# Two of four down groups moved to the end of each layer's last Strassen chunk

## The chip, the cores and the metric

The kernel runs on one core of one Trainium2 chip. The metric is the device time of one execution in microseconds (us). The time before is 2076.21 us, the median of 3 runs (2076.1 to 2077.36).

## What is computed

The program is a two-layer encoder over 256 tokens of width 2048, in float32. Layer 0 mixes tokens with a convolution module, layer 1 with latent attention; behind each mixer stands a feed-forward block of inner width 5632. Cut to what matters:

```python
def swiglu(h, w_gate, w_up, w_down):
    return (jax.nn.silu(h @ w_gate) * (h @ w_up)) @ w_down

for i in range(DEPTH):                      # DEPTH = 2
    h = h + mixer_i(rmsnorm(h, attn_norm_g[i]))
    h = h + swiglu(rmsnorm(h, ffn_norm_g[i]), ffn_w_gate[i], ffn_w_up[i], ffn_w_down[i])
return rmsnorm(h, final_norm_g)
```

## The kernel before

Every float32 product is made of three products of rounded halves: high by high, high by low, low by high. A weight group is 128 partitions x 2048 elements (1 MB). SP loads it into a tile (four slots of `raw`, and `row_bc` as a fifth), ScalarE (ACT) makes the high half in `w_hi` (L687), VectorE (DVE) makes the low half in `w_lo` (L874), and TensorE (PE) multiplies (L1367). `w_hi` and `w_lo` have four slots each, used in turn, so the ACT split of a group waits until PE has used the group four places before it.

The feed-forward block runs over 11 chunks of 512 inner columns. Chunk 0 is plain. In each of chunks 1 to 10 the first two quarters of the gate and up products are made by Strassen's scheme with seven products (Q1 to Q7, 12 matmuls each), the other quarters plainly (G2, G3 for gate, U2, U3 for up, 24 matmuls each, 12 for each of the two token tiles), and in between stand the four down groups D0 to D3 (24 matmuls each) that multiply the hidden activations of the chunk before. The order on PE is written out by hand in `chunk` and, as positions, in the list at L89: Q1, Q3, (transposes of the hidden activations of the chunk before), Q5, D0, D1, Q6, D2, Q7, D3, Q2, G2, Q4, G3, U2, U3. ACT and DVE follow orders of their own, also written out by hand. An engine's queue runs strictly in order.

These dependencies touch the change:

- Q5, Q7, Q6 and Q4 use sums of a gate and an up weight group. POOL issues a DMA that adds the second weights onto the first ones where they lie in `raw` (L530). The sum for Q4 is added where Q6's sum lies, so it is issued once DVE has made the low half of Q6.
- After Q6, DVE mixes Strassen results in the PSUM banks (`mix_q1_q6`, L1172 to L1177); Q7 waits for the second of these.
- After Q7, ACT copies bank 1 (`q167`, L740) and DVE subtracts it from bank 3 (`mix_q7`, L1181). PE waits for that (`mixed`, 4n+4) ahead of G2, which goes on writing into banks 0 and 1.
- The results of a down group are added to the residual by DVE (`add`, L1147), two additions a group; each counts in `out_added`. The four groups use PSUM banks 4 to 7 in turn: D0 4 and 5, D1 6 and 7, D2 4 and 5, D3 6 and 7.
- `hidden(c)` on PE transposes the hidden activations into banks 4 and 5. It waits for the whole of `up_mul(c)` (L1139) and, for each bank, for the addition that empties it:

```python
pe.wait_ge(ff_h_done, 4 * (FC * l + c) + 4)
for b in range(2):
    pe.wait_ge(out_added, added + TT * CC * (c - 1) + 5 + b)
```

  With 8 additions a chunk this is the fifth and the sixth one made in the chunk that the down groups of c-1 stand in: those of D2. ACT then copies the transposes into `a_hi` (L716), DVE makes `a_lo` (L1121), and only then the next down group starts.
- Behind chunk 10 PE has `hidden(10)` and then the four last down groups, whose weights are at the positions F_LAST to F_LAST + 3, here FL0 to FL3.

Of the kernel before, what the change touches and what calls it, by code (L numbers as in the profile page):

```python
# [87 lines left out]

Q1, Q3, Q5, D0, D1, Q6, D2, Q7, D3, Q2, G2, Q4, G3, U2, U3 = range(15)  # L89
DOWN = (D0, D1, D2, D3)  # L90
F_CHUNK = 15
F_FIRST = 2 * KG
F_LAST = F_FIRST + F_CHUNK * (FC - 1)
F_ALL = F_LAST + CC
F_RAW = {Q1: 0, Q5: 0, Q6: 0, Q4: 0, Q3: 1, Q7: 1, D0: 4, D1: 2, D2: 3, D3: 4, Q2: 2, G2: 3, G3: 4, U2: 2, U3: 3}


def f_pos(c, p):
    return F_FIRST + F_CHUNK * (c - 1) + p


def f_part(q):
    return (q - F_FIRST) % F_CHUNK


def f_raw(q):

    if q < F_FIRST:
        return q % RING
    return F_RAW[f_part(q)] if q < F_LAST else q - F_LAST  # L110


def f_w(q):
# [45 lines left out]
def encoder(nc, x, positions, attn_norm_g, ffn_norm_g, final_norm_g, conv_w_pw1, conv_b_pw1, conv_w_dw,  # L159
# [3 lines left out]
    with ctx:  # L163
# [192 lines left out]
        def wait_f_lo(eng, l, q):  # L356
            eng.wait_ge(f_lo_done, F_ALL * l + q + 1)

        def wait_f_used(eng, l, q):
            eng.wait_ge(f_used, F_ALL * l + q + 1)  # L360

        def chunk_no(l, c):

            return (FC - 1) * l + c - 1
# [31 lines left out]
        def _(sp):  # L396
# [46 lines left out]
            def ffn_loads(l):  # L443
                wg, wu, wd = ffn_w_gate[l], ffn_w_up[l], ffn_w_down[l]

                def f_load(q, src):
                    before = f_before(q, f_raw)
                    if before is not None:
                        wait_f_lo(sp, l, before)
                    elif q < RING:  # L450
                        wait_lo(sp, G_END[l] - RING + q)
                    elif l == 0:
                        sp.wait_ge(out_added, TT)
                    sp.dma_start(f_raw_tile(l, q).rearrange("p (k n) -> p k n", k=GK), src).then_inc(f_in[f_raw(q)], 16)

                def part(c, p):
                    f_load(f_pos(c, p), w_of(l, p, c))

                for n, w in ((0, wg), (1, wu)):
                    for j in range(KG):  # L460
                        f_load(KG * n + j, tile_rows(w, slice(GK * j, GK * j + GK), slice(0, CH)))
                part(1, Q1)
                part(1, Q3)
                for p in (D0, D1, D2):
                    part(1, p)
                for c in range(1, FC):
                    for p in (D3, Q2, G2):
                        part(c, p)
                    if c < FC - 1:
                        part(c + 1, Q3)  # L470
                    for p in (G3, U2, U3):
                        part(c, p)
                    if c < FC - 1:
                        part(c + 1, Q1)
                        for p in (D0, D1, D2):
                            part(c + 1, p)
                for n in range(CC):
                    f_load(F_LAST + n, w_of(l, DOWN[n], FC))
            ffn_loads(0)

            for j in range(KG):
# [83 lines left out]
        def _(act):  # L565
# [134 lines left out]
            def ffn(l):  # L700

                def gate_sig(c):

                    for t in range(TT):
                        if c > 0 and t == 0:
                            act.wait_ge(tile0_done, 2 * chunk_no(l, c) + 1)
                        else:
                            wait_f_used(act, l, KG - 1 if c == 0 else f_pos(c, G3))
                        act.activation(ff_sig[:, t, :], ps[:, t, :], ACT.Sigmoid,
                                       scale=rstd[:, t:t + 1]).then_inc(ff_sig_done, 1)  # L710

                def hidden(c):

                    for b in range(2):
                        act.wait_ge(ff_tr, 2 * (FC * l + c) + b + 1)
                        act.activation(a_hi[:, 0, 2 * b:2 * b + 2, :].rearrange("p k s -> p (k s)"), ps[:, 4 + b, :],  # L716
                                       ACT.Copy).then_inc(ahi_done, 1)

                def parts_hi(c, *parts):
                    for p in parts:  # L720
                        f_hi(l, f_pos(c, p))

                for q in range(3, F_FIRST):
                    f_hi(l, q)
                act.wait_ge(rstd_ready, RSTD[(2, 5)[l]])
                act.wait_ge(s_sum_done, l + 1)
                act.activation(s_hi[:, :, :, :].rearrange("p n k s -> p (n k s)"), ytmp[:, 1, :],
                               ACT.Copy).then_inc(s_hi_done, 1)
                gate_sig(0)
                parts_hi(1, Q1, Q3, Q5)  # L730
                for c in range(1, FC):
                    parts_hi(c, D0, D1)
                    wait_f_used(act, l, f_pos(c, Q1))
                    act.activation(q1, ps[:, 0, :], ACT.Copy).then_inc(q1_done, 1)
                    hidden(c - 1)
                    wait_f_used(act, l, f_pos(c, Q5))
                    act.activation(q5, ps[:, 3, :], ACT.Copy).then_inc(q5_done, 1)
                    parts_hi(c, Q6, D2, Q7, D3, Q2, G2)
                    wait_f_used(act, l, f_pos(c, Q7))
                    act.activation(q167, ps[:, 1, :], ACT.Copy).then_inc(q167_done, 1)  # L740
                    parts_hi(c, Q4, G3, U2, U3)
                    parts_hi(c + 1, 0)
                    gate_sig(c)
                    if l == 1 and c == FC - 1:
                        wait_f_lo(act, l, f_pos(c, G3))
                        act.dma_start(row_bc[:, :], final_norm_g.rearrange("(a d) -> a d", a=1).to_broadcast([P, D])
                                      ).then_inc(final_g_in, 16)
                    parts_hi(c + 1, 1, 2)
                hidden(FC - 1)
                f_hi(l, F_ALL - 1)  # L750
                if l == 0:

                    end = G_DQ
                    hi(end)
                    chunk_hi(3, 0, R_ATTN + KT)
                    hi(end + 1)
                    chunk_hi(3, 1, R_ATTN + KT)
                    hi(end + 2)
# [99 lines left out]
        def _(dve):  # L858
# [257 lines left out]
            def ffn(l):  # L1116
# [79 lines left out]
                for c in range(1, FC):  # L1196
                    parts_lo(c, D0, D1)
                    hidden(c - 1)
                    parts_lo(c, Q6, D2)
                    add(0, f_pos(c, D0))  # L1200
                    parts_lo(c, Q7)
                    add(1, f_pos(c, D1))
                    mix_q1_q6(c)
                    parts_lo(c, D3, Q2)
                    add(2, f_pos(c, D2))
                    parts_lo(c, G2)
                    mix_q7(c)
                    parts_lo(c, Q4)
                    add(3, f_pos(c, D3))
                    parts_lo(c, G3, U2, U3)  # L1210
                    parts_lo(c + 1, 0)
                    gate_mul(c)
                    parts_lo(c + 1, 1)
                    up_mul(c)
                    parts_lo(c + 1, 2)
                hidden(FC - 1)
                end = G_DQ
                f_lo(l, F_ALL - 1)
# [141 lines left out]
        def _(pe):  # L1360
# [140 lines left out]
            def ffn(l, x_count, added):  # L1501
# [73 lines left out]
                def chunk(c):  # L1575

                    n = chunk_no(l, c)
                    h = 4 * (FC * l + c - 1)
                    pe.wait_ge(ff_h_done, h + 2)
                    strassen(c, Q1, 0, x_tile(0, 0), first=True)  # L1580
                    pe.wait_ge(ff_h_done, h + 3)
                    pe.wait_ge(s_done, l + 1)
                    strassen(c, Q3, 2, s_tile(4), first=True)
                    hidden(c - 1)
                    strassen(c, Q5, 3, s_tile(1), first=True)
                    down(c - 1, 0, f_pos(c, D0))
                    down(c - 1, 1, f_pos(c, D1))
                    strassen(c, Q6, 1, s_tile(2), first=True)
                    down(c - 1, 2, f_pos(c, D2))
                    pe.wait_ge(mixed, 4 * n + 2)  # L1590
                    strassen(c, Q7, 1, s_tile(3))
                    down(c - 1, 3, f_pos(c, D3))
                    pe.wait_ge(q1_done, n + 1)
                    strassen(c, Q2, 0, x_tile(1, 0))
                    pe.wait_ge(mixed, 4 * n + 4)
                    plain(c, G2, 0, 2)
                    strassen(c, Q4, 1, x_tile(1, 1))
                    plain(c, G3, 0, 3)
                    plain(c, U2, 2, 2)
                    plain(c, U3, 2, 3)  # L1600

                def down_last(added):

# [218 lines left out]
```

## Time and profile before

| | before |
|---|---|
| median of 3 runs | 2076.21 us |
| the profiled execution | 2076.16 us |
| span from its first to its last instruction | 2074.3 us |
| PE busy | 2022.3 us, 97% |
| DVE busy | 1472.8 us, 71% |
| ACT busy | 937.0 us, 45% |
| mean granted TensorE clock | 0.992 |

Busy shares are means over the whole span. The difference of 1.86 us between the profiled execution's own time and its span lies outside the instructions. In timeline rows the columns are start, duration, engine, line, operation, tiles, and in brackets the idle time of the engine before it and what ended it. Matmul rows last longer than the distance between two of them, since matmuls are pipelined: the distance of the starts is what one costs.

### The profile page before, as it was taken

To read this page: it belongs to the slowest core of one execution; us is meant where nothing else is said; L and a number is where in the kernel's file an instruction comes from. 1 tells how busy PE (TensorE), PEld (TensorE's weight loads), DVE (VectorE), ACT (ScalarE), POOL (GpSimd) and SP (SyncE) were. 2 spreads that over 40 slices of the span, in tenths; PEclk is the share of its full clock that TensorE was granted. 3 is DMA by queue.
4 is the path that set the end of the run, shared out by engine and by line. 5 is a ranking of instruction groups with operands and counts; after the bars stand their busy time and mean duration, and the time that the engine had idled before them with its cause. 6 is when DMAs were issued, how large, how long until landed. Compare 5 with 4: busy or idle time off the path is not lost.

```text
span 2074.3 us, 23536 instructions
## 1 busy us (share of the span) xinstructions
PE 2022.3 (97%) x9570; PEld 1705.0 (82%) x9570; DVE 1472.8 (71%) x1727; ACT 937.0 (45%) x847; POOL 124.3 (6%) x105
## 2 busy tenths in 40 slices
PE   6999989999999999999989999999999999999996
PEld 6888878888888888888878998888888888888885
DVE  2999986777667777667657775477766767766764
ACT  3000263554554455545445554355455545454543
POOL 0000000000000000000001000000000000000001
PEclk9999999999999999999999999999999999999998
DMA  6544436689889989898844534668988999889981
GB/s 210 160 144 149 156 129 221 180 269 247 228 233 254 274 260 238 216 265 254 244 142 137 150 129 143 201 182 266 247 220 242 252 275 264 229 220 261 262 245 61
DMA packets 251461, 438.59 MB, mean 211 GB/s; under 512 B 18140, under 2 KB 59876, under 8 KB 250852
## 3 DMA queue, kind: packets, MB, share of 16 engines
q1 hardware_dynamic: 207648, 349.73, 48.4%
q0 software_dynamic: 42240, 83.89, 24.0%
q10 hardware_dynamic: 1476, 3.61, 0.5%
q8 instruction: 69, 1.13, 0.2%
q14 instruction: 28, 0.23, 0.0%
HBM read 435.10 MB, written 2.10 MB: 211 GB/s over the span
## 4 chain that ended last, share of the span: by engine, by line
PE 89%; DVE 7%; DMA 1%; ACT 1%; issue 1%; ACTq 0%; DVEq 0%
PE ps L1367 86%; DVE w_lo L874 2%; DVE scratch L975 2%; DMA raw<-in_ffn_w_up_dram 1%; PE ps L1556 1%; DMA scratch<-in_conv_w_dw_dram 1%; PE ps L1757 0%; PE ps L1758 0%; PE ps L1738 0%; ACT w_hi L687 0%; DVE w_lo L869 0%; DVE x_lo L901 0%; PE ps L1411 0%; PE ps L1400 0%; DVE scratch L1156 0%
## 5 line engine op out<-in xcount | busy, mean ns | idle before, releaser
L874 DVE TENSOR_TENSOR w_lo<-raw,w_hi 128x2048 fp32r<-128x2048 f32 x264 | 601.6, 2287 | 277.9 <-ACT w_hi L687 277.8
L687 ACT ACTIVATE w_hi<-raw 128x2048 fp32r<-128x2048 f32 x264 | 500.9, 1914 | 485.0 <-PE ps L1367 198.3
L1367 PE MATMUL ps<-w_hi,x_hi 128*128 128x512 f32 x1328 | 518.0, 390 | 2.7 <-DVE x_lo L1021 1.8
L1367 PE MATMUL ps<-w_hi,x_lo 128*128 128x512 f32 x1328 | 516.7, 389 | 0.0
L1367 PE MATMUL ps<-w_lo,x_hi 128*128 128x512 f32 x1328 | 516.7, 389 | 0.0
L1367 PE MATMUL ps<-w_hi,a_hi 128*128 128x512 f32 (+1 forms) x768 | 294.5, 384 | 2.8 <-DVE a_lo L1121 2.8
L1367 PEld LDWEIGHTS ps<-w_hi,x_hi 128*128 128x128 f32 x1328 | 249.3, 188 | 55.7 <-issue 1.7
L1367 PE MATMUL ps<-w_lo,a_hi 128*128 128x512 f32 (+1 forms) x768 | 293.8, 383 | 0.0
L1367 PE MATMUL ps<-w_hi,a_lo 128*128 128x512 f32 (+1 forms) x768 | 293.5, 382 | 0.0
L1367 PEld LDWEIGHTS ps<-w_hi,x_lo 128*128 128x128 f32 x1328 | 249.3, 188 | 51.9
L1367 PEld LDWEIGHTS ps<-w_lo,x_hi 128*128 128x128 f32 x1328 | 249.3, 188 | 51.7
L1367 PE MATMUL ps<-x_f,raw 128*128 128x256 f32 x1024 | 222.2, 379 | 0.0
L1367 PEld LDWEIGHTS ps<-x_f,raw 128*128 128x128 f32 x1024 | 194.0, 190 | 26.1
L975 DVE SCALAR_TENSOR_TENSOR scratch<-scratch,tap_col 128x256 f32<-128x256 f32 x452 | 179.7, 475 | 0.0
L1367 PEld LDWEIGHTS ps<-w_hi,a_hi 128*128 128x128 f32 x768 | 145.5, 189 | 32.1 <-DVE w_lo L874 4.3
L1367 PEld LDWEIGHTS ps<-w_hi,a_lo 128*128 128x128 f32 x768 | 145.6, 190 | 27.9
L1367 PEld LDWEIGHTS ps<-w_lo,a_hi 128*128 128x128 f32 x768 | 145.6, 190 | 27.6
L530 POOL DMA_DIRECT2D raw<-in_ffn_w_up_dram x60 | 77.2, 1286 | 1516.6 <-DVE w_lo L874 1516.6
L687 ACT ACTIVATE w_hi<-row_bc 128x2048 fp32r<-128x2048 f32 x60 | 115.2, 1920 | 97.2 <-PE ps L1367 97.2
L869 DVE TENSOR_TENSOR w_lo<-raw,w_hi 128x2048 fp32r<-128x2048 f32 x57 | 130.1, 2291 | 38.7 <-ACT w_hi L580 38.4
L580 ACT ACTIVATE w_hi<-raw 128x2048 fp32r<-128x2048 f32 x57 | 108.1, 1913 | 86.1 <-PE ps L1367 73.0
L874 DVE TENSOR_TENSOR w_lo<-row_bc,w_hi 128x2048 fp32r<-128x2048 f32 x60 | 137.1, 2284 | 5.6 <-ACT w_hi L687 5.3
(197 smaller groups left out, 1781.9 us busy)
## 6 DMA issues: line engine op xcount, KB each, us to landing
raw<-in_ffn_w_gate_dram SPq DMA_DIRECT2D x68, 1024.0 KB, 9.6
raw<-in_ffn_w_up_dram SPq DMA_DIRECT2D x68, 1024.0 KB, 7.4
raw<-in_ffn_w_up_dram POOLq DMA_DIRECT2D x60, 1024.0 KB, 9.1
raw<-in_ffn_w_down_dram SPq DMA_DIRECT2D x48, 1024.0 KB, 5.5
row_bc<-in_ffn_w_down_dram SPq DMA_DIRECT2D x40, 1024.0 KB, 9.3
raw<-in_conv_w_pw_dram SPq DMA_DIRECT2D x64, 512.0 KB
raw<-in_ffn_w_gate_dram POOLq DMA_DIRECT2D x20, 1024.0 KB, 9.9
row_bc<-in_ffn_w_gate_dram SPq DMA_DIRECT2D x20, 1024.0 KB, 6.7
```

The lines of the kernel that those rows point to most:

```text
L530: pool.dma_start(f_raw_tile(l, q).rearrange("p (k n) -> p k n", k=GK), w_of(l, p, c), accum_op=ALU.add).then_inc(f_added[f_raw(q)], 16)
L580: act.activation(w_hi[:, slot, :], raw[:, slot, :], ACT.Copy).then_inc(hi_done, 1)
L687: act.activation(f_w_tile(w_hi, l, q), f_raw_tile(l, q), ACT.Copy).then_inc(f_hi_done, 1)
L869: dve.tensor_tensor(w_lo[:, g % RING, :], raw[:, g % RING, :], hi32(w_hi[:, g % RING, :]), ALU.subtract).then_inc(lo_dve, 1)
L874: dve.tensor_tensor(f_w_tile(w_lo, l, q), f_raw_tile(l, q), hi32(f_w_tile(w_hi, l, q)), ALU.subtract).then_inc(f_lo_done, 1)
L975: dve.scalar_tensor_tensor(acc[:, m, :], vbuf[:, m, w:w + S], tap_col[:, w, tile:tile + 1], acc[:, m, :], ALU.mult, ALU.add).then_inc(conv ...
L1367: ins = pe.matmul(dst, lhsT, rhs, start=first and n == 0, stop=last and n == len(pairs) - 1, skip_group_check=skip)
L1556: ins = pe.transpose(ps[:, 4 + b, S * kk + P * t:S * kk + P * t + P], ff_h[:, t, P * m:P * m + P], ident[:, :])
```

## The change

In chunk 10 of each layer PE runs D2 and D3 behind U3 and not between Q6 and Q2, and Q2 ahead of Q7. Positions come from a second list, ORDER_LAST. The raw slots of the moved groups change, and with them the order of SP's loads; FL1 and FL0 are loaded ahead of U3 and D2. ACT copies `q167` behind the splits of Q4 and G3, DVE makes `mix_q7` behind the low half of Q4. At the end of the chunk DVE has the low half of FL0, `up_mul`, the low half of FL1, the additions of D2, the low half of FL2, the additions of D3. Chunks 1 to 9 keep their order. In layer 1 the load of the final gain on ACT's queue stands behind the split of FL0.

```diff
 Q1, Q3, Q5, D0, D1, Q6, D2, Q7, D3, Q2, G2, Q4, G3, U2, U3 = range(15)
+ORDER = (Q1, Q3, Q5, D0, D1, Q6, D2, Q7, D3, Q2, G2, Q4, G3, U2, U3)
+ORDER_LAST = (Q1, Q3, Q5, D0, D1, Q6, Q2, Q7, G2, Q4, G3, U2, U3, D2, D3)
+F_RAW_LAST = {**F_RAW, D0: 4, D1: 2, Q2: 3, G2: 4, G3: 2, U2: 3, U3: 4, D2: 2, D3: 3}
...
 # SP
+                c = FC - 1
+                for p in (G2, G3, U2):
+                    part(c, p)
+                last_down(1)
+                part(c, U3)
+                last_down(0)
+                part(c, D2)
+                part(c, D3)
+                last_down(2)
+                last_down(3)
...
 # ACT, last chunk
+                        parts_hi(c, Q6, Q2, Q7, G2, Q4, G3)
+                        q167_out(c)
+                        parts_hi(c, U2, U3, D2)
+                        gate_sig(c)
+                        parts_hi(c, D3)
+                        f_hi(l, f_next(c, 0))
+                        if l == 1:
+                            wait_f_lo(act, l, f_pos(c, U3))
+                            act.dma_start(row_bc[:, :], final_norm_g.rearrange("(a d) -> a d", a=1).to_broadcast([P, D])
+                                          ).then_inc(final_g_in, 16)
+                    for n in (1, 2):
+                        f_hi(l, f_next(c, n))
...
 # DVE, last chunk
+                        parts_lo(c, Q6, Q2)
+                        add(0, f_pos(c, D0))
+                        parts_lo(c, Q7)
+                        add(1, f_pos(c, D1))
+                        mix_q1_q6(c)
+                        parts_lo(c, G2, Q4)
+                        mix_q7(c)
+                        parts_lo(c, G3, U2, U3, D2)
+                        gate_mul(c)
+                        parts_lo(c, D3)
+                        f_lo(l, f_next(c, 0))
+                        up_mul(c)
+                        f_lo(l, f_next(c, 1))
+                        add(2, f_pos(c, D2))
+                        f_lo(l, f_next(c, 2))
+                        add(3, f_pos(c, D3))
...
 # PE
-                    down(c - 1, 2, f_pos(c, D2))
-                    pe.wait_ge(mixed, 4 * n + 2)
-                    strassen(c, Q7, 1, s_tile(3))
-                    down(c - 1, 3, f_pos(c, D3))
-                    pe.wait_ge(q1_done, n + 1)
-                    strassen(c, Q2, 0, x_tile(1, 0))
+                    if c < FC - 1:
+                        down(c - 1, 2, f_pos(c, D2))
+                        q7(c)
+                        down(c - 1, 3, f_pos(c, D3))
+                        q2(c)
+                    else:
+                        q2(c)
+                        q7(c)
                     pe.wait_ge(mixed, 4 * n + 4)
                     plain(c, G2, 0, 2)
                     strassen(c, Q4, 1, x_tile(1, 1))
                     plain(c, G3, 0, 3)
                     plain(c, U2, 2, 2)
                     plain(c, U3, 2, 3)
+                    if c == FC - 1:
+                        down(c - 1, 2, f_pos(c, D2))
+                        down(c - 1, 3, f_pos(c, D3))
```

## Rows read from the trace of the kernel before

**Rows 1.** The page's chain of work that ended last, by engine.

```profile
PE 89%; DVE 7%; DMA 1%; ACT 1%; issue 1%; ACTq 0%; DVEq 0%
```

**Rows 2.** That chain in order of time (start, us, what): chunk 10, layer 0.

```profile
987.36 0.87 PE ps L1556 x8
988.23 57.18 PE ps L1367 x252
```

**Rows 3.** Timeline behind U3 of chunk 10, layer 0, PE, ACT and DVE.

```profile
1045.01 0.39 PE L1367 MATMUL ps<-w_hi,x_lo 128*128 128x512 f32 x1
1045.49 3.71 ACT L687 ACTIVATE w_hi<-raw 128x2048 fp32r<-128x2048 f32 x2 [2.37 <-PE ps L1367]
1047.43 2.29 DVE L874 TENSOR_TENSOR w_lo<-raw,w_hi 128x2048 fp32r<-128x2048 f32 x1 [1.82 <-ACT w_hi L687]
1049.64 1.40 DVE L1139 SCALAR_TENSOR_TENSOR scratch<-ps,rstd,scratch 128x512 f32<-128x512 f32 x2
1050.96 2.28 DVE L874 TENSOR_TENSOR w_lo<-raw,w_hi 128x2048 fp32r<-128x2048 f32 x1
...
1051.10 1.97 PE L1556 MATMUL ps<-ident,scratch 128*128 128x128 f32 x8 [5.71 <-DVE scratch L1139]
...
1053.16 1.28 DVE L1121 TENSOR_TENSOR a_lo<-ps,a_hi 128x512 fp32r<-128x512 f32 x2
...
1053.99 0.76 PE L1367 MATMUL ps<-w_hi,a_hi 128*128 128x512 f32 x1 [0.92 <-DVE a_lo L1121]
...
1059.07 0.39 PE L1367 MATMUL ps<-w_hi,a_hi 128*128 128x512 f32 x1
```

**Rows 4.** Timeline at the same place in layer 1, PE.

```profile
2031.60 0.39 PE L1367 MATMUL ps<-w_hi,x_lo 128*128 128x512 f32 x1
...
2040.58 0.77 PE L1367 MATMUL ps<-w_hi,a_hi 128*128 128x512 f32 x1 [0.92 <-DVE a_lo L1121]
```

**Rows 5.** Stretches: width, PE, PEld, DVE, ACT, POOL busy; granted clock; DMA share, GB/s.

```profile
1048.00:1052.00 4.00, 0.90 (x4) 0.90 (x5) 4.00 (x4) 1.20 (x1) 0.00 (x0) 0.57 0.51 145
...
1056.00:1060.00 4.00, 4.00 (x14) 3.10 (x13) 1.82 (x1) 0.00 (x0) 0.00 (x0) 0.65 0.74 233
```

**Rows 6.** Timeline, PE, first matmul of Q6 and of D2, chunk 10, layer 0.

```profile
1001.71 0.39 PE L1367 MATMUL ps<-w_hi,s_hi 128*128 128x512 f32 x1
...
1004.43 0.39 PE L1367 MATMUL ps<-w_hi,a_hi 128*128 128x512 f32 x1
```

**Rows 7.** Timeline, POOL: issue of Q4's sum in layer 0 and in layer 1.

```profile
1000.12 1.28 POOL L530 DMA_DIRECT2D raw<-in_ffn_w_gate_dram  x1 [13.65 <-DVE w_lo L874]
...
1985.84 1.29 POOL L530 DMA_DIRECT2D raw<-in_ffn_w_gate_dram  x1 [12.76 <-DVE w_lo L874]
```

**Rows 8.** DMA issues, window of layer 0 holding Q4's sum (last column: us to landing).

```profile
raw<-in_ffn_w_gate_dram POOLq DMA_DIRECT2D x1, 1024.0 KB, 10.0
```

**Rows 9.** The page's DMA issues: all Q4 sums, other sums, plain down loads.

```profile
raw<-in_ffn_w_up_dram POOLq DMA_DIRECT2D x60, 1024.0 KB, 9.1
raw<-in_ffn_w_down_dram SPq DMA_DIRECT2D x48, 1024.0 KB, 5.5
...
raw<-in_ffn_w_gate_dram POOLq DMA_DIRECT2D x20, 1024.0 KB, 9.9
```

**Rows 10.** Timeline, ACT: splits of Q6, D2, Q7, then D3's; copy `q167`.

```profile
995.59 5.52 ACT L687 ACTIVATE w_hi<-raw 128x2048 fp32r<-128x2048 f32 x3 [3.96 <-DMA raw<-in_ffn_w_up_dram]
1001.97 1.92 ACT L687 ACTIVATE w_hi<-row_bc 128x2048 fp32r<-128x2048 f32 x1 [0.86 <-PE ps L1367]
...
1013.88 0.58 ACT L740 ACTIVATE scratch<-ps 128x512 f32<-128x512 f32 x1
```

**Rows 11.** Timeline, DVE: additions of D1, second mix, `mix_q7`.

```profile
1005.35 1.28 DVE L1147 TENSOR_TENSOR resid<-resid,ps 128x512 f32<-128x512 f32 x2
...
1007.27 0.69 DVE L1175 TENSOR_TENSOR scratch<-scratch,ps 128x512 f32<-128x512 f32 x1
...
1016.40 0.69 DVE L1181 TENSOR_TENSOR ps<-ps,scratch 128x512 f32<-128x512 f32 x1
```

More of the change, by code:

```diff
@@ L95, with f_next, in_last @@
 F_RAW = {Q1: 0, Q5: 0, Q6: 0, Q4: 0, Q3: 1, Q7: 1, D0: 4, D1: 2, D2: 3, D3: 4, Q2: 2, G2: 3, G3: 4, U2: 2, U3: 3}
+F_RAW_LAST = {**F_RAW, D0: 4, D1: 2, Q2: 3, G2: 4, G3: 2, U2: 3, U3: 4, D2: 2, D3: 3}
 def f_pos(c, p):
-    return F_FIRST + F_CHUNK * (c - 1) + p
+    return F_FIRST + F_CHUNK * (c - 1) + (ORDER if c < FC - 1 else ORDER_LAST).index(p)
+def f_next(c, n):
+    return F_FIRST + F_CHUNK * c + n
+def in_last(q):
+    return q >= F_LAST - F_CHUNK
 def f_part(q):
-    return (q - F_FIRST) % F_CHUNK
+    return (ORDER_LAST if in_last(q) else ORDER)[(q - F_FIRST) % F_CHUNK]
 def f_raw(q):
@@ L109, in f_raw @@
         return q % RING
-    return F_RAW[f_part(q)] if q < F_LAST else q - F_LAST
+    if q >= F_LAST:
+        return q - F_LAST
+    return (F_RAW_LAST if in_last(q) else F_RAW)[f_part(q)]
 def f_w(q):
@@ L465, in ffn_loads, with last_down @@
                     part(1, p)
-                for c in range(1, FC):
+                for c in range(1, FC - 1):
                     for p in (D3, Q2, G2):
                         part(c, p)
-                    if c < FC - 1:
-                        part(c + 1, Q3)
+                    part(c + 1, Q3)
                     for p in (G3, U2, U3):
                         part(c, p)
[L473 to L477, printed above, removed]
-                    f_load(F_LAST + n, w_of(l, DOWN[n], FC))
+                    part(c + 1, Q1)
+                    for p in (D0, D1, D2 if c < FC - 2 else Q2):
+                        part(c + 1, p)
+                def last_down(n):
+                    f_load(F_LAST + n, w_of(l, DOWN[n], FC))
+                c = FC - 1
[8 more added lines that the diff above has]
+                last_down(3)
             ffn_loads(0)
@@ L721, in parts_hi, with q5_out, q167_out @@
                         f_hi(l, f_pos(c, p))
+                def q5_out(c):
+                    wait_f_used(act, l, f_pos(c, Q5))
+                    act.activation(q5, ps[:, 3, :], ACT.Copy).then_inc(q5_done, 1)
+                def q167_out(c):
+                    wait_f_used(act, l, f_pos(c, Q7))
+                    act.activation(q167, ps[:, 1, :], ACT.Copy).then_inc(q167_done, 1)
                 for q in range(3, F_FIRST):
@@ L735, in ffn @@
                     hidden(c - 1)
[L736 to L748, printed above, removed]
+                    q5_out(c)
+                    if c < FC - 1:
+                        parts_hi(c, Q6, D2, Q7, D3, Q2, G2)
+                        q167_out(c)
+                        parts_hi(c, Q4, G3, U2, U3)
+                        f_hi(l, f_next(c, 0))
+                        gate_sig(c)
+                    else:
+                        parts_hi(c, Q6, Q2, Q7, G2, Q4, G3)
+                        q167_out(c)
+                        parts_hi(c, U2, U3, D2)
+                        gate_sig(c)
+                        parts_hi(c, D3)
+                        f_hi(l, f_next(c, 0))
+                        if l == 1:
[4 more added lines that the diff above has]
+                        f_hi(l, f_next(c, n))
                 hidden(FC - 1)
@@ L1198, in ffn @@
                     hidden(c - 1)
[L1199 to L1215, printed above, removed]
+                    if c < FC - 1:
+                        parts_lo(c, Q6, D2)
+                        add(0, f_pos(c, D0))
+                        parts_lo(c, Q7)
+                        add(1, f_pos(c, D1))
+                        mix_q1_q6(c)
+                        parts_lo(c, D3, Q2)
+                        add(2, f_pos(c, D2))
+                        parts_lo(c, G2)
+                        mix_q7(c)
+                        parts_lo(c, Q4)
+                        add(3, f_pos(c, D3))
+                        parts_lo(c, G3, U2, U3)
+                        f_lo(l, f_next(c, 0))
[3 more added lines that the diff above has]
+                        f_lo(l, f_next(c, 2))
+                    else:
+                        parts_lo(c, Q6, Q2)
+                        add(0, f_pos(c, D0))
+                        parts_lo(c, Q7)
+                        add(1, f_pos(c, D1))
+                        mix_q1_q6(c)
+                        parts_lo(c, G2, Q4)
+                        mix_q7(c)
+                        parts_lo(c, G3, U2, U3, D2)
+                        gate_mul(c)
+                        parts_lo(c, D3)
+                        f_lo(l, f_next(c, 0))
+                        up_mul(c)
+                        f_lo(l, f_next(c, 1))
+                        add(2, f_pos(c, D2))
+                        f_lo(l, f_next(c, 2))
+                        add(3, f_pos(c, D3))
                 hidden(FC - 1)
@@ L1588, in chunk @@
                     strassen(c, Q6, 1, s_tile(2), first=True)
-                    down(c - 1, 2, f_pos(c, D2))
-                    pe.wait_ge(mixed, 4 * n + 2)
-                    strassen(c, Q7, 1, s_tile(3))
-                    down(c - 1, 3, f_pos(c, D3))
-                    pe.wait_ge(q1_done, n + 1)
-                    strassen(c, Q2, 0, x_tile(1, 0))
+                    if c < FC - 1:
+                        down(c - 1, 2, f_pos(c, D2))
+                        q7(c)
+                        down(c - 1, 3, f_pos(c, D3))
+                        q2(c)
+                    else:
+                        q2(c)
+                        q7(c)
                     pe.wait_ge(mixed, 4 * n + 4)
@@ L1600, in chunk, with q7, q2 @@
                     plain(c, U3, 2, 3)
+                    if c == FC - 1:
+                        down(c - 1, 2, f_pos(c, D2))
+                        down(c - 1, 3, f_pos(c, D3))
+                def q7(c):
+                    pe.wait_ge(mixed, 4 * chunk_no(l, c) + 2)
+                    strassen(c, Q7, 1, s_tile(3))
+                def q2(c):
+                    pe.wait_ge(q1_done, chunk_no(l, c) + 1)
+                    strassen(c, Q2, 0, x_tile(1, 0))
                 def down_last(added):
```

## The prediction

> **What bounds the kernel now.** I read the page's chain first: 89% of the span is PE [rows 1]. In order of time it shows what kind of PE time that is: in the last chunk of layer 0 one unbroken piece of 252 matmuls takes 57.18 us, 0.227 each, behind 0.87 us of transposes [rows 2]. So inside a chunk PE never waits; splits, additions, mixes and loads all lie beside it. Moving PE work there can win nothing. It can only open a wait.
>
> The one place of this chunk with something to win is behind U3. In layer 0 the last matmul of U3 starts at 1045.01, so PE is free at 1045.24 (call such an end T). ACT can split FL1 only now, since its slot was U3's (T + 0.25). DVE follows with FL1's low half at 1047.43, `up_mul` at 1049.64, FL2's low half at 1050.96, and `a_lo` at 1053.16; the transposes stand at 1051.10, the first down matmul at 1053.99, T + 8.75 [rows 3]. Less the 0.87 that transposes cost anyway, 7.88 us are lost. The stop also costs clock: the granted mean of 0.57 over 1048 to 1052 puts the fall from full (2.4 GHz) to half (1.2 GHz) at 1048.56, 3.3 us after PE stopped, and 0.65 over 1056 to 1060 puts the return at 1058.8 [rows 5]. The first 12 down matmuls take 1059.07 - 1053.99 = 5.08 us where 12 x 0.227 = 2.72 would do: 2.36 us more [rows 3]. Layer 1 is the same: 2031.60 to 2040.58, 8.98 between the two matmul starts as in layer 0 [rows 4]. In all about 20.5 us stand behind the two last chunks.
>
> **The end of the chunk after the change.** D2 and D3 are 48 matmuls, 48 x 0.227 = 10.9 us, moved from mid-chunk to behind U3. They are neither added nor removed, so the end of PE's work in the chunk, T, stands where it did, plus whatever is lost mid-chunk. What follows T depends on the order of DVE.
>
> FL0's slot was D2's, free at T - 5.44. ACT's split starts 0.25 later, its low half on DVE runs from T - 3.25 to T - 1.05, and `up_mul` (1.32 from start to next start) from there to T + 0.27. So the `up_mul` that PE waited for is ready in time; this is the part that would close the gap. But `hidden(10)` also waits for the two additions of D2, and DVE has these behind FL1's low half. FL1's slot is now D3's, free only at T. So: ACT's split at T + 0.25, FL1's low half at T + 2.19 to T + 4.40, as in [rows 3]; additions of D2 to T + 5.60 (two take 1.28 [rows 11], of which 0.08 overlap with the next, as 1.40 shown and 1.32 to the next start do for `up_mul` [rows 3]); FL2's low half 2.20, to T + 7.80; additions of D3, 1.20, to T + 9.00; `a_lo` there; first down matmul 0.83 later, as 1053.16 to 1053.99 in [rows 3]: T + 9.83. The transposes have started at about T + 5.1, one bank after the other, and ACT has copied them by T + 8; they don't decide. That is 1.08 us a layer later than T + 8.75: `up_mul` (1.32) has left the DVE list behind T, but two pairs of additions (2.40) have come into it. PE still stops for over 5 us, so the clock's 2.36 are lost as before (I take no difference; at the ends +1 or -1). Sum for the end: 2 x 1.08 = 2.2 us.
>
> **Mid-chunk.** Here a cover goes. Before, D3 and Q2, 36 matmuls or 8.2 us, stood on PE between Q7 and G2 and hid `q167` and `mix_q7`. Now G2 is next behind Q7. In layer 0 D1 ends at 1001.71 and Q6 at 1004.43 [rows 6]; Q2 then ends at 1007.15 and Q7, if nothing waits, at 1009.87. Q7 waits for the second mix on DVE, which ends at 1007.27 + 0.69 = 1007.96 [rows 11]. DVE's work ahead of it is the same in number and kind (the low half of Q2 in place of D2's), so Q7 starts at 1008.05 and ends at 1010.77.
>
> Before G2 PE waits for `mix_q7`, that for `q167`, and ACT now has the splits of Q4 and of G3 ahead of `q167`. Q4's split needs its sum. POOL issues it once Q6's low half is made, at 1000.12 [rows 7], which the change leaves alone, and it lands 10.0 us later, at 1010.12 [rows 8]. From there: two splits at 1.84 (three take 5.52 [rows 10]) are 3.68; `q167` 0.58 [rows 10]; `mix_q7` 0.69 [rows 11]; three hand-overs of 0.04 between engines: G2 starts 5.07 after the landing. Q4's low half (2.20) runs on DVE in the meantime, done before `q167` is. G2 starts at 1015.19, against 1009.87: 5.32 us lost. G3's split doesn't wait longer (Q2 used its slot by 1007.15), and its load and G2's are issued in the place of D3's and Q2's; the split of D3, in the same slot `row_bc` that G2 now takes, waited for PE and not for a load [rows 10].
>
> In layer 1 all PE times stand 986.59 later (2031.60 - 1045.01, [rows 3, 4]), so G2 would be due at 1996.46. The sum is issued at 1985.84 [rows 7]; with the median 9.9 of all twenty Q4 sums [rows 9] it lands at 1995.74, and G2 starts at 2000.81: 4.35 us lost. Together 9.7 us. Loads behind the sum (U2's and FL1's in place of G2's) come through the same DMA engines; I take the landing as unchanged, and for the bounds 1 us either way in each layer.
>
> These stops are new places for the clock to fall. PE stands for 1015.19 - 1010.77 = 4.4 us in layer 0 and 4.3 in layer 1, longer than the 3.3 after which it fell behind U3. I take a fall in each, at the 2.36 measured: 4.7 us. Lower bound 0, no fall. Upper bound: the whole half-clock spell of 1058.8 - 1048.6 = 10.2 us [rows 5] falls on a busy PE, which then does half its work, 5.1 us each.
>
> **What is free.** The rest of the chunk has room: later splits (U2, U3, D2, D3) wait for PE's slots, not for loads, and PE is later, not they. FL2's load now waits for D2's low half and FL3's for D3's; a load takes about 5.5 us [rows 9], D2's low half is made about 20 us ahead of FL2's split. If that cover were gone each us of lateness would add to T + 9.83. The load of the final gain in layer 1 issues on ACT near T - 3 and is needed at the first final addition, some 14 us later. Chunks 1 to 9 keep their order.
>
> **Sum.** Against the profiled execution's own 2076.16 (within 0.1 of the median 2076.21): 9.7 mid-chunk + 4.7 clock + 2.2 at the ends = 16.6, so 2092.7 us. One per cent here is 20.8 us; 0.2%, about what a measurement of this kernel can tell from no change, is 4.2 us.
>
> **A page's rule.** The Trainium skill, "DMA: Bandwidth & Descriptors", section on the anatomy of one DMA (SWDGE path), gives a GpSimd-issued DMA about 2 us plus its bytes at 436 GB/s; for 1 MB that would be an estimate of 4.4 us. The row of this trace says 10.0, and the trace is taken. By that rule the sum would be that of rival C below, 2082.5.
>
> **Rivals.**
> A. The forecast, 2092.7, with its own range 2090 to 2096: 0.64.
> B. The waits come, but the clock doesn't fall in them: 2076.16 + 9.7 + 2.2 = 2088.1 (2090.4 with one fall). For it: the stops are only 1 us longer than the 3.3. Chance 0.13.
> C. Q4's sum lands early. The mid-chunk wait is then Q7's own chain: `q167` 0.2 behind Q7's end, 0.58, 0.69 and hand-overs, about 1.6 us behind 1010.77 in layer 0 (2.5 lost) and behind 1996.46 in layer 1 (1.6 lost), too short for a fall: 2076.16 + 4.1 + 2.2 = 2082.5. It decides once the sum lands within about 7.2 us of its issue. A plain load does that (5.5), but the two kinds of sums have medians 9.1 and 9.9 [rows 9]. Chance 0.04.
> D. It is worse. The sums land later beside the fuller queue, or the half-clock spells lie wholly on work: up to 2 + 2 x (5.1 - 2.36) = 7.5 more, 2100; typically 2097. Chance 0.12.
> E. The other side: D2 and D3 do cover what follows U3, since `up_mul` is done at T + 0.27. If the additions of D2 didn't hold back the transposes, nor DVE's list `a_lo`, 2 x (7.88 + 2.36) = 20.5 would come back: 2076.16 + 9.7 + 4.7 - 20.5 = 2070.1. It decides only if the additions of D2 and D3 run ahead of FL1's low half, and DVE is in order. Chance 0.04.
> F. Small waits at both places, within 4.2 us of before: 0.03.
>
> Faster by over 0.2% comes from E (0.04), the same from F and the low edge of C (0.04), slower the rest (0.92). The range takes in B and most of D: 2086.0 to 2098.0.
>
> **What would show it.** In the changed trace: a PE gap of about 4.4 us ahead of G2 in both last chunks, its releaser DVE L-line of `mix_q7`, with ACT busy on two splits back to back between the landing of Q4's sum and `q167`; a gap under 1 us ahead of Q7 in layer 0; four stretches at half clock in the feed-forward blocks and not two; D3 end to first down matmul 9.8 us, with transposes starting near T + 5.1. It would be wrong if ACT had Q4's split done before Q7 ended (the sum landing near 1004), or if the transposes started within 1 us of D3's end.

## The result, and the profile after

| | before | changed |
|---|---|---|
| median | 2076.78 us (4 runs, 2076.1 to 2077.54) | 2091.34 us (4 runs, 2090.8 to 2093.73) |
| ratio | | 1.0075, 95% interval 1.0063 to 1.0087 |
| the profiled execution | 2076.16 us | 2093.73 us |
| span | 2074.3 us | 2091.9 us |
| PE busy | 2022.3 us | 2028.9 us |

The change makes the kernel 14.6 us slower by the medians. The profiled execution is the slowest of the four; between the two profiled ones lie 17.6 us. The readings below add up to 17.2 of these. The trace also has PE 0.67 us late at 400 us, long ahead of all changed code, so those 0.67 us do not come from the change.

The page's chain, by engine, answers to [rows 1]: PE falls from 89 to 86%, DVE and DMA rise by 1 and 2 points.

```profile
PE 86%; DVE 8%; DMA 3%; ACT 2%; issue 1%; ACTq 0%; POOL 0%; DVEq 0%; POOLq 0%
```

The points of DMA (59.4 us in the chain after, 30.2 before: what is new are the two Q4 sums below and one sum of another group in layer 1, 9.26 us) are not that much new waiting: the chain is followed back from releaser to releaser, and takes the DMA for the whole time from issue to landing even where PE was busy beside it. In order of time (start, us, what) the chain of the changed kernel through the middle of layer 0's last chunk reads:

```profile
1001.14 10.13 DMA raw<-in_ffn_w_gate_dram
1011.27 0.02 issue
1011.30 1.92 ACT w_hi L711
...
1013.24 2.29 DVE w_lo L913
1015.54 0.70 DVE ps L1220
1016.24 0.04 issue
1016.28 3.78 PE ps L1424 x8
```

Q4's sum lands 10.13 us after its issue, ACT splits it, DVE makes its low half, then `mix_q7`, then G2 starts. The same in layer 1, with 9.64 for the sum:

```profile
1996.25 9.64 DMA raw<-in_ffn_w_gate_dram
...
2010.90 1.19 PE ps L1424 x4
```

The timeline of the same stretches shows what PE lost. Rows are the first matmul of Q7 and of G2 in layer 0, the last of Q7 and the first of G2 in layer 1, and the ACT rows of layer 0:

```profile
1009.03 0.50 PE L1424 MATMUL ps<-w_hi,s_hi 128*128 128x512 f32 x1 [1.04 <-DVE scratch L1214]
...
1011.30 3.71 ACT L711 ACTIVATE w_hi<-raw 128x2048 fp32r<-128x2048 f32 x2 [6.73 <-DMA raw<-in_ffn_w_gate_dram]
1014.91 0.58 ACT L753 ACTIVATE scratch<-ps 128x512 f32<-128x512 f32 x1
...
1016.28 0.80 PE L1424 MATMUL ps<-w_hi,x_hi 128*128 128x512 f32 x1 [4.24 <-DVE ps L1220]
...
2006.89 0.39 PE L1424 MATMUL ps<-w_hi,s_lo 128*128 128x512 f32 x1
...
2010.90 0.50 PE L1424 MATMUL ps<-w_hi,x_hi 128*128 128x512 f32 x1 [3.62 <-DVE ps L1220]
```

In layer 0 PE ended Q2 at 1007.83 (its last matmul starts at 1007.60), waited for the second mix, and waited again behind Q7. Unhindered, G2 would have started 2.72 behind Q2's end, at 1010.55; it started at 1016.28, 5.73 late. In layer 1 only the second wait is there: due at 2007.11, started at 2010.90, 3.79 late. (The idle times in brackets, 4.24 and 3.62, count from the modelled end of the last matmul and are 0.2 shorter than the time between its pace and the next start.)

The end of the chunk, the chain in order of time in layer 0:

```profile
1054.85 1.92 ACT w_hi L711
...
1056.79 2.29 DVE w_lo L913
1059.08 1.19 DVE resid L1186 x2
1060.28 2.20 DVE w_lo L913
1062.48 1.20 DVE resid L1186 x2
1063.67 0.61 DVE a_lo L1160
```

Behind FL1's split come its low half, the additions of D2, FL2's low half, the additions of D3, `a_lo`, on DVE without a pause. The timeline rows around it, PE, answer to [rows 3]:

```profile
1054.36 0.39 PE L1424 MATMUL ps<-w_hi,a_lo 128*128 128x512 f32 x1
...
1059.83 0.44 PE L1613 MATMUL ps<-ident,scratch 128*128 128x128 f32 x1 [5.07 <-DVE resid L1186]
...
1064.42 0.77 PE L1424 MATMUL ps<-w_hi,a_hi 128*128 128x512 f32 x1 [2.66 <-DVE a_lo L1160]
```

D3's last matmul starts at 1054.36, so T is 1054.59 and the first last-down matmul starts at T + 9.83; the transposes waited for the additions of D2, at L1186. Before it was T + 8.75.

The clock, by stretches (width, PE, PEld, DVE, ACT, POOL busy, granted clock, DMA share, GB/s), answers to [rows 5]:

```profile
1015.00:1019.00 4.00, 2.72 (x6) 2.16 (x7) 4.00 (x4) 2.29 (x3) 0.00 (x0) 0.56 1.03 376
1019.00:1024.00 5.00, 5.00 (x17) 3.97 (x16) 1.62 (x1) 0.00 (x0) 0.00 (x0) 0.67 1.03 379
...
1068.00:1072.00 4.00, 4.00 (x15) 3.17 (x14) 0.00 (x0) 0.00 (x0) 0.00 (x0) 0.74 0.86 261
2007.00:2012.00 5.00, 1.38 (x7) 0.93 (x6) 4.14 (x4) 4.91 (x4) 0.00 (x0) 1.00 1.05 393
2012.00:2016.00 4.00, 4.00 (x12) 3.14 (x11) 3.23 (x2) 0.00 (x0) 0.00 (x0) 0.57 1.05 386
```

The clock has two levels here, so a mean between them says how long each was granted: 0.56 over 4 us means half clock (1.2 GHz) from 1015.5; 0.67 over 5 means back to full (2.4 GHz) at 1022.3. G2 ran from 1016.28, so 6.0 us of work went at half rate: 3.0 lost. In layer 1 the clock is full until 2012 (the matmuls start 0.23 apart up to 2012.16 and 0.43 apart behind it) and then at half for 3.4 us, all of it on a busy PE: 1.7 lost. The half-clock spells (stretches at 1.2 GHz) at the ends last to 1070.1 in layer 0 (0.74 over 1068 to 1072): 5.7 us of half-rate work, 2.8 lost where before it was 2.4. Layer 1 is the same, 2.75 against 2.35.

### The profile page after: what moved, and what is told of

It reads as the page before. It is cut to its first block, busy times and chain, and to the rows that moved or that the text cites. A ratio compares the mean times of both kernels' runs of the same rounds, so it can differ in the third digit from the quotient of the medians.

```text
span 2091.9 us, 23536 instructions
## 1 busy us (share of the span) xinstructions
PE 2028.9 (97%) x9570; PEld 1709.3 (82%) x9570; DVE 1473.6 (70%) x1727; ACT 937.0 (45%) x847; POOL 124.3 (6%) x105
## 4 chain that ended last, share of the span: by engine, by line
PE 86%; DVE 8%; DMA 3%; ACT 2%; issue 1%; ACTq 0%; POOL 0%; DVEq 0%; POOLq 0%
PE ps L1424 83%; DVE w_lo L913 3%; DVE scratch L1014 2%; DMA raw<-in_ffn_w_up_dram 1%; DMA raw<-in_ffn_w_gate_dram 1%; PE ps L1613 1%; ACT w_hi L711 1%; DMA scratch<-in_conv_w_dw_dram 1%; PE ps L1827 0%; PE ps L1828 0%; PE ps L1808 0%; DVE w_lo L908 0%; DVE x_lo L940 0%; PE ps L1457 0%; PE ps L1468 0%
## 5 line engine op out<-in xcount | busy, mean ns | idle before, releaser
L913 DVE TENSOR_TENSOR w_lo<-row_bc,w_hi 128x2048 fp32r<-128x2048 f32 x60 | 137.1, 2286 | 14.8 <-ACT w_hi L711 14.6
```

The source lines that it names most:

```text
L913: dve.tensor_tensor(f_w_tile(w_lo, l, q), f_raw_tile(l, q), hi32(f_w_tile(w_hi, l, q)), ALU.subtract).then_inc(f_lo_done, 1)
```

## The experiments

Each ratio is to runs of the kernel before on the same chip (medians 2075.6 to 2076.4 us). The changed kernel's 2091.34 stands beside a before of 2076.78, so a difference between it and a run below is known to about 1 us only. In every run the edits touch the last chunk of each layer and the last down groups behind it alone. "Waits" and "gaps" are PE's idle times as the profile gives them.

**The copy `q167` alone earlier.**

```diff
-                        parts_hi(c, Q6, Q2, Q7, G2, Q4, G3)
-                        q167_out(c)
-                        parts_hi(c, U2, U3, D2)
+                        parts_hi(c, Q6, Q2, Q7, G2)
+                        q167_out(c)
+                        parts_hi(c, Q4, G3, U2, U3, D2)
```

> The changed kernel with one edit in the last chunk: ACT copies q167 ahead of the splits of Q4 and G3; DVE's order stays, with mix_q7 behind the low half of Q4. In the changed kernel's trace the copy ended at 1015.49 and DVE's low half of Q4 at 1015.53, so both orders hold G2 to the landing of Q4's sum. Theory (either order alone is enough to hold it): no change, 2091.3 us within 1.5, gap ahead of G2 still about 4.2 and 3.6 us. Rival (the place of the copy on ACT alone makes the wait): about 2081.

Measured: 2096.46 us, ratio to before 1.0101 (1.0084 to 1.0118), some 5 us slower than the changed kernel. Neither "no change" nor the rival. The gaps ahead of G2 are 5.4 us in both layers, in place of 4.2 and 3.6: 3.0 of the 5 us. Its chain through the middle of layer 1:

```profile
1993.85 12.99 PE ps L1424 x57
...
2006.86 0.02 ACT scratch L753
...
2007.36 1.91 ACT w_hi L711
...
2009.29 2.29 DVE w_lo L913
2011.58 0.62 DVE ps L1220
...
2012.25 2.08 PE ps L1424 x4
```

The DMA has left the chain, PE stands at its head: ACT waits in the copy for Q7 to end and only then, at 2007.36, splits Q4, whose sum was issued at 1995.92 and landed 9.7 us later, at 2005.6. DVE still wants that low half ahead of the mix. So DVE's order was enough to hold the wait, as the theory had it, but the expectation missed that the copy, once ahead, pushes the split behind Q7's end. The other half of the theory, that ACT's order alone would hold it too, was not run.

**Copy and mix both earlier.** As above, and on DVE:

```diff
-                        parts_lo(c, G2, Q4)
-                        mix_q7(c)
-                        parts_lo(c, G3, U2, U3, D2)
+                        parts_lo(c, G2)
+                        mix_q7(c)
+                        parts_lo(c, Q4, G3, U2, U3, D2)
```

> As the run before, and mix_q7 on DVE ahead of Q4's low half as well. Theory: G2 waits only for Q7's own chain (copy, mix), some 1.6 us behind Q7's end, G2 is 2.5 us late in layer 0 and 1.6 in layer 1 in place of 5.7 and 3.8, and the two half-clock spells (3.0 and 1.7 us lost) go: 2091.3 - 3.2 - 2.2 - 4.7 = 2081 us. Rival (the moved PE groups or the changed loads make the wait by themselves): stays above 2088.

Measured: 2082.86 us, 1.0036 (1.0022 to 1.0051). PE's waits mid-chunk in layer 0 (waiting line, releaser, us, times, longest):

```profile
PE ps L1424 <- DVE scratch L1214: 1.4, 1, 1.4
PE ps L1424 <- DVE ps L1220: 1.4, 1, 1.4
```

The gap ahead of G2 is 1.4 us in each layer, plus 1.4 ahead of Q7 in layer 0, and the granted clock stays at 1.00 mid-chunk in both. With PE's order untouched, the orders of ACT and DVE gave back 8.5 of the 14.6 us by the medians, 7.3 if each is held against the kernel before of its own chip.

**Q4's sum as a plain load.**

```diff
-                    for p in (Q5, Q7, Q6, Q4):
+                    for p in (Q5, Q7, Q6, Q4) if c < FC - 1 else (Q5, Q7, Q6):
                         add(c, p)
...
-                for p in (G2, G3, U2):
+                for p in (G2, G3, Q4, U2):
                     part(c, p)
```

> The changed kernel, but in the last chunk of each layer Q4's group is a plain load of the gate weights on SP's queue in place of POOL's added sum, so the up weights are left out of it; all orders stay. A plain load takes about 5.5 us in place of 10. Theory (the landing of Q4's sum, through ACT's and DVE's orders, makes the mid-chunk wait): mid-chunk as in the run with copy and mix early, G2 2.5 and 1.6 us late, no half-clock spell there, 2082 us. Rival (the splits themselves, two on ACT and one on DVE ahead of copy and mix, make it): 2088 or more.

Measured: 2086.96 us, 1.0054 (1.0038 to 1.0071), between the two. This kernel leaves out the up weights in Q4, so it is read for its times alone. The load landed 5.3 us after its issue in layer 0, 5.2 in layer 1. Its chain through the middle of layer 0:

```profile
1008.90 0.70 DVE scratch L1214
...
1009.62 0.70 DVE ps L1216
1010.32 4.39 DVE w_lo L913 x2
1014.71 0.62 DVE ps L1220
...
1015.37 1.66 PE ps L1424 x6
```

With the sum out of the way the wait ahead of G2 is 2.7 us in each layer, and what makes it is DVE's own list: the low halves of G2 and of Q4 (4.39) between the first mixes and `mix_q7`. By the medians the landing is worth 4.4 us (2091.34 to 2086.96) and the orders, once the group lands early, 4.1 (2086.96 to 2082.86): both theory and rival hold a part. Gaps of 2.7 us brought no fall of the clock, the granted mean stays at 1.00.

**The additions of D2 earlier.**

```diff
                         parts_lo(c, D3)
+                        add(2, f_pos(c, D2))
                         f_lo(l, f_next(c, 0))
                         up_mul(c)
                         f_lo(l, f_next(c, 1))
-                        add(2, f_pos(c, D2))
                         f_lo(l, f_next(c, 2))
                         add(3, f_pos(c, D3))
```

> The changed kernel with one edit at the end of the chunk: DVE makes the additions of D2 ahead of FL0's low half, not behind FL1's. Theory (DVE's list up to a_lo sets the first down matmul, the additions of D2 only the transposes): transposes start 0.4 us behind D3's end in place of 5.1, first down matmul at T + 8.6 in place of T + 9.8: 2091.3 - 2.4 = 2089 us. Rival (the additions of D2 are what holds the end): the 5 us before the transposes come back in each layer, with clock 2080 or less.

Measured: 2090.81 us, 1.0068 (1.0051 to 1.0085); the single times run from 2087.4 to 2091.9, so its distance to the changed kernel's 2091.34 is not told apart from none by the times. Its chain at the end of layer 0's chunk settles the theory:

```profile
1054.47 1.92 ACT w_hi L711
...
1056.41 4.49 DVE w_lo L913 x2
1060.90 1.20 DVE resid L1186 x2
1062.10 0.61 DVE a_lo L1160
```

The transposes now wait only 0.3 us, but PE stops 7.1 us behind them for `a_lo`, and the first last-down matmul starts at T + 8.6, as expected. DVE's list up to `a_lo` holds the end, not the additions of D2 as such.

**The hidden step ahead of FL1 and FL2 as well.** The edit is shown against the run just above.

```diff
 # DVE
                         up_mul(c)
+                        hidden(c)
                         f_lo(l, f_next(c, 1))
-                        f_lo(l, f_next(c, 2))
                         add(3, f_pos(c, D3))
+                        f_lo(l, f_next(c, 2))
-                hidden(FC - 1)
...
 # ACT
+                    if c == FC - 1:
+                        hidden(c)
                     for n in (1, 2):
                         f_hi(l, f_next(c, n))
-                hidden(FC - 1)
```

> As the run before, and ACT's a_hi copies and DVE's a_lo of the last chunk ahead of the splits of FL1 and FL2. Theory: first down matmul at T + 2.6, 7.2 us earlier in each layer, and no half-clock spell at the ends (2.8 us each): 2091.3 - 20 = 2071 us. Rival (the splits of FL1 and FL2 are needed soon enough to give it back): a new wait ahead of the second down group, 2080 or more.

Measured: 2073.18 us (10 runs), 0.9989 (0.998 to 0.9999). PE's waits at the end of layer 0's chunk are two:

```profile
PE ps L1425 <- DVE a_lo L1161: 1.1, 1, 1.1
PE ps L1614 <- DVE scratch L1179: 0.3, 1, 0.3
```

There is no half-clock spell behind them, and no new wait ahead of the second down group. The gain of 18.2 us over the changed kernel is near the 20 expected. What DVE and ACT had ahead of `a_lo` made the stop.

**Both places mended.** The edits of the run with copy and mix earlier, and those of the run just above.

> The changed kernel's order on PE, with the mid-chunk orders of the run with copy and mix early and the end orders of the run with the hidden step early. Theory (two separate waits, both made by the orders of ACT and DVE): mid-chunk 2.5 and 1.6 us late, ends 1.5 us each, no half-clock spell in the feed-forward blocks: the 20.5 us of before less 4.1 and 3.0, 2075.6 - 13.4 = 2062 us. Rival (the two waits share a cause): the sum of the two single gains is not reached, 2070 or more.

Measured: 2063.85 us, 0.9944 (0.9927 to 0.9961). The single gains were 8.5 and 18.2, their sum 26.7, and 27.5 were measured. Held against the kernel before of their own chips the three are 7.3, 17.0 and 27.1. So the rival, a shared cause, which would leave the sum unreached, is out; how exactly the two add up is known to some 3 us. What is left in layer 0 is short, these two and 0.3 us twice:

```profile
PE ps L1425 <- DVE ps L1221: 1.4, 1, 1.4
PE ps L1425 <- DVE a_lo L1161: 1.1, 1, 1.1
```

**The kernel before, ACT and DVE reordered at the end, nothing moved on PE.**

```diff
 # ACT, as in the run before; DVE:
-                    parts_lo(c + 1, 1)
-                    up_mul(c)
+                    if c < FC - 1:
+                        parts_lo(c + 1, 1)
+                        up_mul(c)
+                    else:
+                        up_mul(c)
+                        hidden(c)
+                        parts_lo(c + 1, 1)
                     parts_lo(c + 1, 2)
-                hidden(FC - 1)
```

> The kernel before, PE's order and all loads unchanged. In the last chunk DVE makes up_mul ahead of FL1's low half, and ACT's a_hi copies and DVE's a_lo stand ahead of the splits of FL1 and FL2. Theory (the wait behind U3 was made by the order of ACT and DVE, not by a lack of PE work): first down matmul 3.1 us behind U3's end in place of 8.75, no half-clock spell: 2075.6 - 16 = 2060 us. Rival (PE work behind U3 is needed to hide the step): within 5 us of before.

Measured: 2063.73 us, 0.9939 (0.9922 to 0.9955), 3.7 slower than expected. PE's waits there, the same in both layers:

```profile
PE ps L1561 <- DVE scratch L1140: 1.6, 1, 1.6
PE ps L1372 <- DVE a_lo L1122: 1.1, 1, 1.1
```

The first down matmul starts 3.9 us behind U3's end (1045.86 to 1049.77, and 2026.51 to 2030.41), not 3.1: `up_mul` starts on DVE at 1046.15 only, behind FL0's low half and the gate's multiplication. That is 0.8 us in each layer. And in layer 0 a half-clock spell of 3.4 us still came, from 1049.7 to 1053.1, 1.7 us of it lost. The two make 3.3 of the 3.7. This run does on ACT and DVE alone what the run before does with two groups moved: within the uncertainty the two are equal.

**D3 alone behind U3, whole.** PE's order is Q1, Q3, Q5, D0, D1, Q6, D2, Q7, Q2, G2, Q4, G3, U2, U3, D3, transposes. Copy and mix stand ahead of Q4's split, the additions of D2 mid-chunk as before, and at the end:

```diff
 # DVE
+                        parts_lo(c, D3)
+                        up_mul(c)
+                        f_lo(l, f_next(c, 0))
+                        hidden(c)
+                        add(3, f_pos(c, D3))
+                        f_lo(l, f_next(c, 1))
+                        f_lo(l, f_next(c, 2))
```

> As the run with D3 halved, but D3 whole behind U3 and the transposes behind D3, with one buffer for the hidden activations (they can be overwritten only once D3 is done). Theory: up_mul is hidden by D3 and D2's banks are long free, so only transposes to a_lo stay open, 1.1 us a layer as in the runs with the hidden step early: 2.2 us over the halved form's 2056.2, so 2058.5 us. Rival (D2 too must be moved to cover up_mul and the split of FL0): 2062 or more, with a wait ahead of the transposes.

Measured: 2059.05 us, 0.992 (0.9903 to 0.9937). The one wait left behind the last chunk is 1.1 us for `a_lo`, in each layer, and the clock stayed full behind it.

**D3 halved around the transposes.** The same, with `a_hi[:, 1]` and `a_lo[:, 1]` for the last hidden activations:

```diff
-                        down(c - 1, 3, f_pos(c, D3))
+                        down(c - 1, 3, f_pos(c, D3), (0,))
+                        hidden(c)
+                        down(c - 1, 3, f_pos(c, D3), (1,))
```

> Before's order on PE up to Q7, then Q2, and D3 alone behind U3, halved: first token tile, transposes of the last chunk, second token tile; the last hidden activations go into the second half of a_hi and a_lo, so that D3 can still read the first. Copy q167 and mix_q7 ahead of Q4's split; FL0's split, a_hi, a_lo, D3's additions, FL1, FL2 at the end. Theory: Q2 (2.7 us) hides copy and mix (1.6), half a D3 hides up_mul, the other half a_hi and a_lo, so PE doesn't stop at all: 2075.6 - 20.5 = 2055 us. Rival (something else, a load or the low half of FL1, holds the last down groups next): 2060 or more.

Measured: 2056.21 us (2055.2 to 2056.92), 0.9907 (0.989 to 0.9923): 20 us faster than before, 35 faster than the changed kernel, and the fastest of all. Its chain through the last chunk of layer 0:

```profile
987.69 27.21 PE ps L1429 x120
1014.90 0.03 issue
1014.93 27.50 PE ps L1429 x120
1042.43 0.87 PE ps L1618 x8
1043.31 13.65 PE ps L1429 x60
```

PE only, but for 0.2 us at G2, which starts when `mix_q7` is done (1014.88) and not at 1014.75: 120 matmuls to G2, 120 more, the transposes in their 0.87, and 60 at the 0.227 of full clock, past the place where PE used to stop.

## Why the prediction was right

It was: 2092.7 forecast, 2091.34 measured, and both waits came where and as it said. That the two totals lie so close is in part luck: the terms were forecast at 16.6 us and come to 17.2 in the profiled execution, but the medians differ by 14.6 only. By its terms, against the profiled execution:

| term | forecast | in the profile |
|---|---|---|
| G2 late, layer 0 and layer 1 | 5.3 + 4.35 | 5.7 + 3.8 |
| clock, mid-chunk | 2.36 + 2.36 | 3.0 + 1.7 |
| first last-down matmul later | 1.08 + 1.08 | 1.08 + 1.07 |
| clock at the ends, more than before | 0 | 0.4 + 0.4 |
| sum | 16.6 | 17.2 of 17.6 |

The kernel before lost 2.4 and 2.35 us to the clock at the ends; the last row but one is what came on top.

- **Mid-chunk.** The step "G2 starts 5.07 after the landing" came out at 5.01 in both layers (1011.27 to 1016.28, 2005.89 to 2010.90). What was off is the start of Q4's sum, issued, against the chunk's own start, 0.35 us later in layer 0 than before and 0.24 earlier in layer 1, and landings of 10.1 and 9.6 for 10.0 and 9.9. That the splits ahead of copy and mix turn the landing into a wait is shown from both sides: with both orders mended 1.4 us are left ahead of G2, with a 5.3 us load 2.7. The wait ahead of Q7 in layer 0 was 1.04 us, where a gap under 1 was named.
- One link was named wrongly. The prediction put the way from landing to mix through ACT's two splits and the copy, with Q4's low half "in the meantime, done before". In the profile the low half ended last, at 1015.53, against 1015.49 for the copy. The two are equal to 0.04 us, so the sum held; but the first experiment, which moved the copy alone, shows that the low half on DVE, which the prediction took for free, holds G2 with the copy out of the way.
- **The clock.** Rival B (no fall) is out: both waits brought one. The size 2.36 was right only as the mean of 3.0 and 1.7, and that is luck: the spells lasted 6.8 us in layer 0 and 3.4 in layer 1. In layer 0 the clock fell 3.6 us after PE had stopped, in layer 1 about 5, when PE was already working again. The term that was put at nothing, more clock at the ends, was 0.8.
- **The end.** T + 9.83 was forecast and measured. That DVE's list up to `a_lo` sets it, and the additions of D2 only the transposes, is shown by the run with the additions alone moved. Rival E's 20.5 us behind the two chunks were there to be had, but not by the condition that it named, the additions of D2 and D3 ahead of FL1's low half: with those of D2 there nothing clear of noise was gained, and the 18.2 us came once `a_hi` and `a_lo` stood ahead of FL1's and FL2's splits and low halves, with the additions of D3 still behind FL1's low half.
- **Rival C** put the time with an early landing at 2082.5 by letting the wait be Q7's own chain. The plain load gave 2086.96: with the sum early, DVE's low halves of G2 and Q4 still stand ahead of the mix, which that rival had left out. Its number is met by the run with both orders mended, 2082.86. On the rule that the prediction cites from the Trainium skill, "DMA: Bandwidth & Descriptors", anatomy of one DMA: by it a 1 MB DMA from GpSimd takes an estimated 4.4 us; the accumulating ones took 10.1 and 9.6, so the trace does not agree with it for this kind of transfer.

Left open: why the profiled execution is 2.4 us over the median of its kernel, so which of the terms a typical run has less of; and what decides whether a stop of 1.6 and 1.1 us with transposes in between brings a half-clock spell (layer 0 of the reordered kernel before) or not (its layer 1).

## What to carry to other kernels

Work moved on the bottleneck engine covers a wait only if the other engines' in-order lists are moved with it: for each wait, list what stands ahead of the releasing instruction on its engine and when each of those is released. Of the 20 us here, 12.6 came back without moving anything on the bottleneck engine, once the step it waited for stood ahead of splits that nobody needed yet; one down group as cover, cut in two around the transposes and with a second buffer for the hidden activations, did the rest. Count also what the moved work used to hide at its old place; two short steps behind Q7 cost 14.2 us with their clock once a slow DMA came to stand ahead of them in an order.

## What the runs showed of the hardware

- A fall of the clock can arrive after the wait is over: PE stopped at 2007.1, resumed at 2010.9, and the granted clock went to half at about 2012.1.
- Stops of 2.7 us ahead of G2 left the clock full in both layers, those of 3.6 to 5.4 us (eight, in four kernels) did not. At the end of a chunk two stops of 1.6 and 1.1 us around transposes brought a short spell in one layer and none in the other.
- Accumulating 1 MB DMAs from GpSimd took about 10 us to land where a plain load of the same size from SP, at the same place of the chunk, took 5.3 and 5.2. Whether the adding or the queue makes it was not separated.
- The plain loads issued 2 and 5 us behind it were late with it: 9.9 and 9.2 us to landing beside the accumulating DMA in layer 0, 6.1 and 6.0 at nearly the same distances behind the plain one.
